# A mixture of experts on one core: the experts' rows summed on chip instead of scattered

## The reference

```python
logits = xn @ router_w + router_b
top_v, top_e = lax.top_k(logits, 4)
gates = softmax(top_v)
# for each expert, its tokens' rows:
h = x @ w_gate_up[e] + b_gate_up[e]          # 1024 x 2048
gate = minimum(h[:, ::2], 7); up = clip(h[:, 1::2], -7, 7)
y = ((up + 1) * (gate * sigmoid(1.702 * gate))) @ w_down[e] + b_down[e]   # 1024 x 1024
# out[token] += gate weight * y, over the token's 4 experts
h = rmsnorm(h + moe(hn))
```

## Time and profile before

| | us |
|---|---|
| time, median of 3 runs | 1773.86 (1773.05 to 1775.25) |
| time of the profiled execution | 1772.09 |
| its span in the profile | 1770.1 |
| PE busy | 1655.0 (93%) |
| VectorE, ACT, POOL busy | 446.5, 364.9, 197.5 |
| DMA, whole span | 500.15 MB, 283 GB/s |

### The profile page before, as it was taken

How to read it: one execution, slowest core, us unless ns; L and a number is a source line. 1 busy time by engine, 2 the same in 40 slices (tenths; PEclk the granted TensorE clock), 3 DMA queues, 4 the chain that set the end, 5 groups by cost and what they waited for, 6 DMA issues and landing times.

```text
span 1770.1 us, 34121 instructions
## 1 busy us (share of the span) xinstructions
PE 1655.0 (93%) x14875; PEld 947.5 (54%) x14876; DVE 446.5 (25%) x704; ACT 364.9 (21%) x649; POOL 197.5 (11%) x170
## 2 busy tenths in 40 slices
PE   9999999999999998999989898999889988998896
PEld 7877778898888883334333343333333333343333
DVE  4147255527323552311100110100010110010013
ACT  4244222238421240101010010011010101010002
POOL 1000000000000004112011102012102110211201
PEclk9999999999999999999999999999999999999998
DMA  5321254421334397999999999999999999999993
GB/s 191 128 82 62 72 166 120 117 72 38 119 97 143 127 394 273 366 381 396 386 397 382 394 403 392 386 393 398 390 390 398 393 387 395 383 394 399 392 368 137
DMA packets 109153, 500.15 MB, mean 283 GB/s; under 512 B 16520, under 2 KB 26720, under 8 KB 59408
## 3 DMA queue, kind: packets, MB, share of 16 engines
q1 hardware_dynamic: 92416, 479.15, 70.5%
q0 software_dynamic: 15536, 16.72, 4.6%
q10 hardware_dynamic: 1056, 2.16, 0.6%
HBM read 480.33 MB, written 19.58 MB: 282 GB/s over the span
## 4 chain that ended last, share of the span: by engine, by line
SPq 26%; PE 20%; DMA 13%; issue 2%; DVE 0%; POOL 0%; ACT 0%; DVEq 0%; POOLq 0%
SPq L1775 22%; PE psum L1977 12%; DMA bias_rows<-biases_hi_lo 9%; PE psum L1986 5%; SPq L1769 4%; DMA expert_chunk_late<-in_expert_w_down 2%; DMA expert_chunk_late<-in_expert_w_gate_up 2%; DMA h_sb<-normed_rows,row_index 1%; PE psum L1994 1%; SPq L1852 1%; PE psum L1950 1%; PE psum L1970 0%; PE psum L1939 0%; PE psum L277 0%; DVE expert_chunk L2117 0%
## 5 line engine op out<-in xcount | busy, mean ns | idle before, releaser
L1977 PE MATMUL psum<-expert_chunk_late,rowsT 128*32 128x512 f32 x2592 | 288.0, 594 | 8.5 <-DMA expert_chunk_late<-in_expert_w_gate_up 8.5
L1977 PE MATMUL psum<-expert_chunk,rowsT 128*32 128x512 f32 x2592 | 288.9, 596 | 6.0 <-DMA expert_chunk<-in_expert_w_gate_up 6.0
L2061 DVE TENSOR_SCALAR gate_values<-psum 128x768 f32<-128x768 f32 (+1 forms) x32 | 27.5, 858 | 907.7 <-PE psum L1977 907.7
L1931 POOL DMA_INDIRECT residual_rows<-h_sb,piece_row x81 | 125.7, 1552 | 858.2 <-ACT h_sb L2042 780.5
L1977 PEld LDWEIGHTS psum<-expert_chunk_late,rowsT 128*32 128x32 f32 x2592 | 80.2, 110 | 187.7 <-issue 170.7
L1977 PEld LDWEIGHTS psum<-expert_chunk,rowsT 128*32 128x32 f32 x2592 | 80.5, 110 | 184.9 <-issue 172.4
L323 DVE TENSOR_TENSOR chunk_lo<-chunk,chunk_hi 128x2048 fp32r<-128x2048 f32 x48 | 110.0, 2291 | 257.7 <-ACT chunk_hi L319 239.3
L1986 PE MATMUL psum<-expert_chunk_late,activationsT 128*32 128x256 f32 x2688 | 165.5, 404 | 2.6 <-DMA expert_chunk_late<-in_expert_w_down 2.6
L1986 PE MATMUL psum<-expert_chunk,activationsT 128*32 128x256 f32 x2496 | 151.2, 399 | 7.7 <-DMA expert_chunk<-in_expert_w_down 7.7
L354 PE MATMUL psum<-xT_hi,chunk_hi 128*128 128x512 f32 x384 | 150.3, 391 | 4.2 <-ACT att_qT_window L1135 1.7
L354 PE MATMUL psum<-xT_lo,chunk_hi 128*128 128x512 f32 x384 | 149.5, 389 | 0.0
(11 more groups left out here) (293 smaller groups left out, 1471.2 us busy)
## 6 DMA issues: line engine op xcount, KB each, us to landing
expert_chunk<-in_expert_w_gate_up SPq DMA_DIRECT2D x132, 1024.0 KB
expert_chunk_late<-in_expert_w_gate_up SPq DMA_DIRECT2D x124, 1024.0 KB
expert_chunk_late<-in_expert_w_down SPq DMA_DIRECT2D x68, 1024.0 KB
expert_chunk<-in_expert_w_down SPq DMA_DIRECT2D x60, 1024.0 KB
chunk<-in_w_in SPq DMA_DIRECT2D x38, 1024.0 KB, 5.2
chunk<-in_w_branch_gla SPq DMA_DIRECT2D x4, 1024.0 KB, 5.1
chunk<-in_w_mix_out SPq DMA_DIRECT2D x4, 1024.0 KB, 5.1
gla_v<-in_x SPq DMA_DIRECT2D x4, 512.0 KB
```

Of the source, the lines that this page charges most:

```text
L1931: pool.indirect_dma_start(pieces, bass.IndirectOffsetOnAxis(ap=self.piece_row[u][:, j:j + 1], axis=0), y[:, j * PIECE:(j + 1) * PIECE], No ...
L1977: last = pe.matmul(bank[part_rows(p), :], x[:, k, part_rows(j)], w[:, p // 2, p % 2 * COLS:(p % 2 + 1) * COLS], start=False, stop=(k == KT ...
L2061: dve.tensor_scalar(by_row(gv), gates_ups(e)[:, :, :, :, 0], SWIGLU_LIMIT, None, ALU.min).then_inc(S["gu"], 1)
```

## The change

1. The sums of the experts' rows stay on chip, turned: `totalT` holds 1024 columns as 8 x 128 partitions, by 512 tokens. The scatter is gone. ACT writes the weighted rows rounded to the fast format (`rows_hi`), VectorE the rest (`rows_lo`), and VectorE compares the pieces' tokens with 0 to 511 (`tokens_of`). PE multiplies both parts with that one-hot matrix (`sum_rows`): operands of 32 rows, one for each quarter of the columns, in the four row groups and into banks 3, 4, 5 and 7, in two halves behind q = 2 and q = 5 of the next body. VectorE adds each half to `totalT` (`add_rows`).
2. VectorE's list and index copies for place e + 2 stand behind both `add_rows`.
3. The activations are turned behind q = 0 and 1 (place 0 as before).
4. Ring of 13 instead of 16, for the memory of `totalT`, the one-hot matrix and the token row; two chunks are no longer loaded ahead of the experts' stage but by the common loop.
5. Every second ordered place has 64 slots: 15 instead of 12.
6. SP loads the bias rows of place e + 2 at q = 5 of body e.
7. At the end the residual is loaded without waiting for a scatter; PE turns `totalT` by products with the identity (`turned_total`) and adds it in the banks.

```diff
-GROUPS_AT = tuple((FEW_SLOTS if p in range(ORDERED.start, ORDERED.stop) and (p - ORDERED.start) % 5 in (0, 2) else FIRST_SLOTS) // 32
+GROUPS_AT = tuple((FEW_SLOTS if p in range(ORDERED.start, ORDERED.stop) and (p - ORDERED.start) % 2 == 0 else FIRST_SLOTS) // 32
-    RING = 16
+    RING = 13
...
+        sum_banks = [self.bank[n] for n in (3, 4, 5, 7)]
+        def rows_hi(act, e):
+            act.wait_ge(S["used"], self.body_chunk(e, BODY - 1) + 1)
+            act.wait_ge(S["pieces"], 2 * e + 2)
+            if e:
+                act.wait_ge(S["rows_summed"], 2 * e)
+            for j in range(GROUPS[e]):
+                act.activation(y_hi[:, j * PIECE:(j + 1) * PIECE], y_of(j), ACT.Copy,
+                               scale=self.piece_weight[e % self.BUFFERS][:, j:j + 1]).then_inc(S["rows_hi"], 1)
+        def rows_lo(dve, e):
+            for j in range(GROUPS[e]):
+                at = slice(j * PIECE, (j + 1) * PIECE)
+                dve.wait_ge(S["rows_hi"], BEFORE[e] + j + 1)
+                dve.scalar_tensor_tensor(out=y_lo[:, at], in0=y_of(j), scalar=self.piece_weight[e % self.BUFFERS][:, j:j + 1],
+                                         in1=y_hi[:, at].bitcast(F32), op0=ALU.mult, op1=ALU.subtract).then_inc(S["rows_lo"], 1)
+        def tokens_of(dve, e):
+            n = GROUPS[e]
+            if e:
+                dve.wait_ge(S["rows_summed"], 2 * e)
+            dve.wait_ge(S["pieces"], 2 * e + 2)
+            dve.tensor_tensor(token_hot[:, 0:n, :], self.token_row[:].unsqueeze(1).to_broadcast([P, n, SEQ]),
+                              self.piece_token[e % self.BUFFERS][:, 0:n].unsqueeze(2).to_broadcast([P, n, SEQ]),
+                              ALU.is_equal).then_inc(S["token_hot"], 1)
+        def sum_rows(pe, e, half, turns):
+            n = GROUPS[e]
+            if half == 0:
+                pe.wait_ge(S["rows_lo"], BEFORE[e + 1])
+                pe.wait_ge(S["token_hot"], e + 1)
+                pe.wait_ge(S["aT_out"], turns)
+            else:
+                pe.wait_ge(S["total_added"], 4 * (2 * e + 1))
+            for x in (y_hi, y_lo):
+                for j in range(n):
+                    for p in range(PARTS):
+                        at = j * PIECE + half * P
+                        last = pe.matmul(sum_banks[p], x[part_rows(p), at:at + P], token_hot[part_rows(p), j, :],
+                                         start=(x is y_hi and j == 0), stop=(x is y_lo and j == n - 1))
+            last.then_inc(S["rows_summed"], 1)
+        def add_rows(dve, e, half):
+            dve.wait_ge(S["rows_summed"], 2 * e + half + 1)
+            for p in range(PARTS):
+                to = totalT[:, 2 * p + half, :]
+                if e == 0:
+                    last = dve.tensor_copy(to, sum_banks[p])
+                else:
+                    last = dve.tensor_tensor(to, to, sum_banks[p], ALU.add)
+                last.then_inc(S["total_added"], 1)
...
         def body_pe(pe, e):
...
                         if e:
-                            pe.wait_ge(S["y_out"], BEFORE[e])
+                            pe.wait_ge(S["total_added"], 8 * e)
-                if q == 2:
+                first_turn = 2 if e == 0 else 0
+                if q == first_turn:
                     turn_act(pe, e, range(2))
-                if q == 3:
+                if q == first_turn + 1:
                     turn_act(pe, e, range(2, GROUPS[e]))
+                if e and q == 2:
+                    sum_rows(pe, e - 1, 0, BEFORE[e] + 2)
+                if e and q == 5:
+                    sum_rows(pe, e - 1, 1, 0)
...
         def body_act(act, e):
             if e:
+                rows_hi(act, e - 1)
...
-            rows_out(act, e)
...
         def body_dve(dve, e):
             more = e < E - 2
+            if e:
+                rows_lo(dve, e - 1)
+                add_rows(dve, e - 1, 0)
+                add_rows(dve, e - 1, 1)
             if more:
                 u = (e + 2) % self.BUFFERS
                 if e > 1:
-                    dve.wait_ge(S["scattered"], 16 * BEFORE[e - 1])
+                    dve.wait_ge(S["gathered"], 16 * (e - 1))
                 at = bass.ds(self.expert_in(dve, e + 2), 1)
                 list_take(dve, at, u)
                 pieces_take(dve, at, u)
             else:
                 list_hot(dve, E - 1)
+            tokens_of(dve, e)
             swiglu(dve, e + 1, self.body_chunk(e, GU - 1))
...
+        def turned_total(pe, b):
+            for k in range(KT):
+                at = slice(k % HALF_KT * P, (k % HALF_KT + 1) * P)
+                pe.matmul(sums[b][:, k // HALF_KT, at], totalT[:, k, b * P:(b + 1) * P], self.ident[:], start=False, stop=False)
...
+                def next_place(sp, e):
+                    at_place.append(self.expert_in(sp, e))
+                    self.load_bias_rows(sp, at_place[e], e)
...
+                        if q == 5 and 0 < e < E - 2:
+                            next_place(sp, e + 2)
...
-                    scatter(pool, e, e % self.BUFFERS)
...
                 for q in range(4):
                     last_down_chunk(pe, self.body_chunk(LAST, q), q)
+                    if q == 0:
+                        sum_rows(pe, LAST - 1, 0, BEFORE[E])
+                    if q == 1:
+                        sum_rows(pe, LAST - 1, 1, 0)
...
+                    if q == 2:
+                        pe.wait_ge(S["weights_out"], 1)
+                        pe.wait_ge(S["total_added"], 8 * LAST)
+                        pe.wait_ge(S["hotT"], 1)
+                        for b in range(3):
+                            bias_products(pe, b)
+                            turned_total(pe, b)
```

More of the change, by code:

```diff
@@ L228, in build @@
                     self.bias_in = [self.sem(f"bias_rows_in{u}") for u in range(2)]
-                    later = [self.sb(moe, f"expert_chunk_late{j}", [P, 2, self.WIDE]) for j in range(self.RING - self.GU)]
+                    later = [self.sb(moe, f"expert_chunk_late{j}", [P, 2, self.WIDE]) for j in range(4)]
+                    self.totalT = self.sb(moe, "added_rowsT", [P, KT, SEQ])
+                    later.append(self.sb(moe, "expert_chunk_late4", [P, 2, self.WIDE]))
+                    self.token_hot = self.sb(moe, "tokens_one_hot", [P, self.GROUPS, SEQ], F32R)
+                    self.token_row = self.sb(moe, "token_row_sb", [P, SEQ])
                     self.rowsT = self.sb(moe, "rowsT", [P, KT, FIRST_SLOTS])
@@ L255, in build @@
                     self.index = [self.sb(moe, f"row_index{u}", [P, 1], I32) for u in range(self.BUFFERS)]
-                    self.piece_row = [self.sb(moe, f"piece_row{u}", [P, self.GROUPS], I32) for u in range(self.BUFFERS)]
+                    self.piece_token = [self.sb(moe, f"piece_token{u}", [P, self.GROUPS]) for u in range(self.BUFFERS)]
                     self.piece_weight = [self.sb(moe, f"piece_weight{u}", [P, self.GROUPS]) for u in range(self.BUFFERS)]
@@ L259, in build @@
                         "tables_in", "weight_rows", "weights_turned", "used", "gu", "sig", "p", "act", "act_turned", "aT_out",
-                        "y_out", "scattered", "hot", "listed", "none", "index", "pieces", "gathered", "x_turned", "x_out",
+                        "rows_hi", "rows_lo", "token_hot", "rows_summed", "total_added", "hot", "listed", "none", "index", "pieces", "gathered", "x_turned", "x_out",
                         "cleared", "passed", "weights_out", "hot_turned", "hotT", "y_hi", "y_lo", "totals", "table_cleared",
-                        "records", "placed", "lists_in", "ordered", "all_pieces", "last_weight", "half_set", "summed", "squared", "means",
+                        "records", "placed", "lists_in", "ordered", "last_weight", "half_set", "summed", "squared", "means",
                         "powed", "done")}
@@ L265, in build @@
                     self.out_stored = self.sem("out_stored")
-                    self.total_sb = [self.expert_ring[b // 2][:, b % 2, :] for b in range(NB)]
+                    self.first_idle = N_EXPERTS * self.PER_BODY - self.RING
+                    self.total_sb = [self.expert_ring[(self.first_idle + b // 2) % self.RING][:, b % 2, :] for b in range(NB)]
                     with self.stage() as s:
@@ L1384, in _ @@
                 sp.wait_ge(self.bank_full[NB - 1], last_mix + 1)
-                for q in range(3, 6):
+                for q in range(3, 5):
                     self.load_gate_up(sp, self.body_chunk(0, q), 1, q)
@@ L2034, in gate_sigmoid, with body_act @@
             act.activation(held(sg, e), held(gv, e), ACT.Sigmoid, scale=SWIGLU_ALPHA).then_inc(S["sig"], 1)
-        def rows_out(act, e):
-            act.wait_ge(S["used"], self.body_chunk(e, BODY - 1) + 1)
-            act.wait_ge(S["pieces"], 2 * e + 2)
+        def body_act(act, e):
             if e:
-                act.wait_ge(S["scattered"], 16 * BEFORE[e])
-            for j in range(GROUPS[e]):
```

(8 more changed lines are left out.)

74 lines of the change are left out of this document (23 added, 51 removed).

## The result

The changed kernel takes 1848.26 us (median of 4 runs, 1846.23 to 1850.79) beside 1774.0 (4 runs, 1773.05 to 1775.25) of the kernel before: the ratio is 1.0416, interval 1.0403 to 1.0428. The forecast was 1791, range 1742 to 1832: the direction was right, the size was not. The profiled execution's span is 1846.9 us, 76.8 more than before.

What follows compares the result with a forecast made beforehand. PE was taken to lead until its 16 chunks in hand ran out, then the weight stream. With the change, 28 bodies +5.6, body 1 +3.5, body 30 -0.5 and tail +8.7 made +17.3 us: 1791, range 1742 to 1832.

Steps and rivals of the forecast that it cites:

- The mechanism: Index cast behind the second sums delays POOL's gather; PE waits for its rows, so freed DMA time buys nothing; chance 0.52.
- PE waits 2.3 us in every body: Wait for gathered rows after chunk 9: 11.3 us from chunk 6 to landing, against PE's 9.0 us of other work.
- nearer 1.00: Sign expected in the profile after: PE's granted clock closer to 1.00, with none of the 54 us for bias rows.
- 7.5 us in every body: Gather's time from POOL's start until its rows land, taken as one value between the rows' 7 to 8 and 14.60.
- Body 1: First `body_pe` pass (eight gate-up chunks of the next expert, four down of this): from 29.2 to 32.7 us, +3.5.
- three signs of being wrong: Gather wait missing, the middle's DMA share staying at 1.02, or four row products taking clearly more than 0.3 us.
- a set of four row products: Four 32-row products of `sum_rows` on four row groups: taken as 0.26 us, between 0.226 and 0.43.
- PE's pair of bodies: PE's own work for two bodies with the new sums, without waits: 56.13 + 20 x 0.26 + 4 x 0.2 = 62.1 us.
- The tail: Kernel's end: last row sums, bias and identity products put 7.2 us on PE's way to the last chunk; +8.7 in all.
- The row groups: Rival: row products hold each other up; 0.43 us a set gives 1839, 0.91 in turn gives 1973; chance 0.09.
- The gather in time: Rival: gather takes 5.2 us or less from POOL's start, PE never waits, bodies near 31.3 us; about 1730; chance 0.30.
- the engines may go idle when the ring is full: Argument for a faster gather: DMA engines may idle with a full ring; that rival gave about 1730, chance 0.30.

Runs made afterwards that it cites:

- e1: Changed kernel with VectorE taking the list and pieces of place e + 2 ahead of the sums; 1743.42 us, 0.9817 of the kernel before.
- e2: Changed kernel with 14 unused products ahead of PE's wait for the gathered rows in every body; 1848.2 us, 1.0413 of the kernel before.
- e7: Changed kernel with the one-hot compare behind swiglu instead of beside POOL's gather instruction; 1820.38 us, 1.0297 of the kernel before.
- e6: Kernel before with each scatter DMA replaced by a semaphore increment, the experts' sums left out; 1731.34 us, 0.9752 of the kernel before.
- e5: Kernel before with only 15 places of 64 instead of 12; 1.0003 of the kernel before.
- e8: Kernel before with only a ring of 13 chunks instead of 16, two chunks no longer loaded ahead of the experts' stage; 1.0034 of the kernel before.
- e9: Kernel before with only the bias rows loaded at chunk 5 of the body before; 0.999 of the kernel before.
- e3: Changed kernel with every gather asking for 64 rows, rows past 64 left out; 1838.56 us, 1.0356 of the kernel before.

## Why the prediction was wrong

**The mechanism held.** It named the cast behind the sums, the chain to POOL, the gather as PE's wait, and that the freed DMA time would then buy nothing. e1 takes that one order away and the time goes from 1.0416 to 0.9817.

**The step that failed** is "PE waits 2.3 us in every body ... A body is then 31.1 + 2.3 = 33.4 us". A pair of bodies was put at 66.7 us. The one shown is 70.4: 62.15 of PE's own (e1), 0.22 + 4.89 of waits, and 3.0 at the low clock (0.1 is left). Two terms were off.

- *The clock was left out.* Of the 28 bodies' 990.2 us, 14 x 62.15 = 870.1 are PE's own and 79.5 waits; 40.6 are left. Taken body by body, the 14 long waits (3.9 to 5.3 us) cost 1.6 to 3.3 us each behind them, 34.9 in all; the two longest of the other kind, 2.13 and 3.25 us, cost 3.3 and 1.8; the other twelve bodies show 0.05 to 0.08. With 2.8 in body 1 that is 43 of the missing 60 us. The forecast even had the clock "nearer 1.00", because it thought of the bias waits as gone, not of what a new wait does. The row was there: with 81 us of idle in 28 bodies the granted clock was 0.96, and in bodies 2 and 3 without a wait 1.00. e2 takes the effect away in 11 of 15 bodies. The Trainium skill states the direction, that idle gaps between matmuls return the clock to its lower level (TensorE: Matmul & The Clock Gate, section "HAM oscillation — how this bites in real kernels"); by that rule, e1, e2 and the kernel after agree. Whether waits of 2.3 us in every body, as forecast, would have cost the clock too, the rows don't settle: one of 2.13 us did, one of 2.93 in e7 did not. So this error hangs in part on the next one.
- *The gather was put too short, and as one value.* 7.5 us in every body became a median of 6.0 and one of 9.9, and 8.2 as the mean of the 29. The time that PE had for it came out as forecast, 5.3 us against 5.2, and no gather was shorter than that (the least wait is 0.22), so the waits add up as the mean says: 83.9 us, 2.9 a body, where 29 x 2.3 = 66.7 were forecast: 17 us. That they are uneven, 0.22 and 4.89 where 2.3 and 2.3 were written, costs by the clock. Some 0.6 us of the long ones' surplus is the compare beside POOL (e7), which the prediction costed at VectorE's delay to swiglu alone.

With these, 17.3 + 43 + 17 = 77, beside 76.8; what differs otherwise (the start, body 30, the tail) comes to about 1 us.

**Body 1**, forecast +3.5, came to +8.3: its wait is 4.42 us instead of 2.3, and 2.8 are lost behind it at the low clock. None of the three signs of being wrong came; they asked for the mechanism, not for the sizes.

**What came out as worked out:** a set of four row products 0.27 us, against 0.26 (by the 3.07 times of the Trainium skill, TensorE: Matmul & The Clock Gate, section "Measured speedup vs the span model", it would have been an estimated 0.29; the prediction has 0.30); PE's pair of bodies 62.15, against 62.1; the scatter 1.6 us a body of the stream (e6), against 1.5; the stream without it 32.1 us a body (e6), against 32.2; POOL's start 3.5 us behind chunk 6, against 3.8. The ends: two halves of row products of 1.14 us (2.3, forecast 2.5), and the bias and identity products in the tail as below, 7.15 us from the first of them (1818.58) to the last chunk's start (1825.73), against 7.2. The tail is +7.6 in all, forecast +8.7. Places, ring and bias rows are worth 0, +6 and 0 (e5, e8, e9).

```profile
1809.18 0.74 PE L1967 MATMUL psum<-tokens_one_hot,last_rows_hi 32*128 32x512 f32 x8
1809.75 0.65 PE L1967 MATMUL psum<-tokens_one_hot,last_rows_lo 32*128 32x512 f32 x8
...
1818.58 1.02 PE L2144 MATMUL psum<-down_bias_hi_lo_hi,weightsT_hi_hi_lo 96*128 96x512 f32 x2
...
1825.73 3.60 PE L2040 MATMUL psum<-expert_chunk,rowsT 128*96 128x512 f32 x8
```

**The rivals.** The row groups don't hold each other up. The gather in time was forecast at 1730 and is e1, at 1743.42: it does happen, but through the order on VectorE and not through a faster DMA, and with 32.0 instead of 31.3 us a body: the stream took the lead back after body 12, not after 26. The chunks in hand were fewer than the forecast's 11: from the start of body 2 (770.4) to PE's first wait for a chunk, in body 13 (1132.4), the hardware queue of e1 moved 140.8 MB, some 134 chunks, while PE came to its 141st. So about seven were in hand, an estimate from these bytes. What the forecast said for this rival, that the engines may go idle when the ring is full, came in every second body of the kernel after, and the gathers there are the short ones. One reading stands askew without bearing on the sum: in the first fourteen slices 38 to 191 GB/s are moved, so the stream's 366 to 403 are mostly three times that or more, not twice.

**Why a gather in every second body takes 3.9 us more.** No run was made for this, but the traces of e1 and e7 hold the comparison. In both nothing holds POOL's instruction up (0.95 us), and a gather of 64 rows is 80 packets. In e7 the DMA engines are part idle in the 2 us around its start (median share 0.65), in e1 they are full (1.00). The software queue in the first 5.2 us from POOL's start, e7 (1209.8 to 1215.0) and e1 (1139.4 to 1144.6):

```profile
q0 software_dynamic: 77, 0.23, 16.5%
...
q0 software_dynamic: 34, 0.14, 8.9%
```

The last packet ends 5.1 us after POOL's start in e7 (median of 14) and 7.8 in e1: full engines account for 2.7 us of the 3.9. The row count has 0.7 (e3) and the compare 0.6 (e7), which makes 4.0. Within the even bodies of e3 and e7 it shows again: the four gathers that met a share of 0.90 or more took 7.4 to 8.1 us to the last packet. One in the kernel after took 8.1 at 0.65, so the share at the start isn't all of it. The idle time comes with the body: in the even one shown SP had issued a chunk by 1221.2 and issues the next at 1225.19, since in the ring of 13 it waits for PE to use one, and half of the engines' time stays empty; in the odd one, chunks are issued 1.4 us before POOL's start and 0.3 behind it.

**Open:** why four of e2's bodies still lost 1.6 to 1.8 us behind waits of 1.6 to 2.4, and why a wait of 2.13 us cost the clock in the kernel after where one of 2.93 in e7 did not.

## What to carry to other kernels

When work is added to an engine, look for the small instruction behind it that starts a DMA, and move that instruction ahead of the work: here a cast of 0.15 us in the wrong place was worth 6% of the kernel. Price a new wait one kind of body at a time, and add what the granted clock costs behind it: here all of the long waits cost the clock, and most of the short ones nothing. A wait's releaser in a stream that leads is only the last in the queue; removing it moves the wait.

## What the runs showed of the hardware

- Behind 4.89 us without a product the granted clock was 0.66 over the next 9.46 us, 3.0 us lost; behind 0.22 us there was no such loss. All 14 waits of 3.9 to 5.3 us in the 28 bodies cost 1.6 to 3.3 us behind them.
- POOL's indirect DMA instruction takes 0.95 us by itself (e7), 1.28 beside a 1024 column compare with two SBUF inputs and 1.80 beside a 1536 column one.
- A gather of 64 rows of 4 KB has its last packet 5.1 us after POOL's start where the DMA engines are part idle at that start (e7, median share 0.65) and 7.8 us where they are full (e1); 96 rows take 8.5 us with full engines (e1).
- The accumulating scatter of a body, 64 tokens' rows on average in pieces of 1 KB, costs the weight stream 1.6 us a body: 392 GB/s with it, 402 without (e6).
- Four products of 32 rows by 512 columns on four row groups take 0.27 us a set, where one full product takes 0.226.
